# Token halves at the seams, three weight slots and roots on PSUM columns in a two-layer hybrid encoder

## The reference, cut to what matters

```python
h = rms_norm(x, ln_pre_mix[l])
m = hybrid_mixer(h, ...)       # combined projection, mixers A, B, C, D, gates, w_out
x = x + rms_norm(m, ln_post_mix[l])
h = rms_norm(x, ln_pre_ffn[l])
gu = h @ ffn_w_gu[l]
f = (silu(gu[..., :D_FF]) * gu[..., D_FF:]) @ ffn_w_down[l]
x = x + rms_norm(f, ln_post_ffn[l])
```

## Time and profile before

| | |
|---|---|
| median of 3 runs | 1854.29 us (1853.89 to 1854.39) |
| profiled execution | 1853.21 us |
| its span, first to last instruction | 1851.4 us |
| mean granted PE clock | 0.971 |
| busy: PE / DVE / ACT / POOL | 1719.6 / 921.1 / 406.1 / 1131.7 us |
| mean DMA rate | 82 GB/s |

### The profile page before, as it was taken

The page is one execution under the profiler, slowest core; times in us unless marked ns, Lnnn a source line. Parts: engine busy times, 40 slices in busy tenths (PEclk is TensorE's granted clock), DMA queues, the critical chain, the costliest instruction groups (busy, mean ns, idle before and its releaser), DMA issues.

```text
span 1851.4 us, 21177 instructions
## 1 busy us (share of the span) xinstructions
PE 1719.6 (93%) x8162; PEld 1404.2 (76%) x8162; DVE 921.1 (50%) x1621; ACT 406.1 (22%) x875; POOL 1131.7 (61%) x1172
## 2 busy tenths in 40 slices
PE   7999999899879999999879999998999699999996
PEld 6778678677667888888677787786776588888885
DVE  5755754865555333410277557558654644343102
ACT  3440313223231111100134313023332211111000
POOL 6536456343666887877584373653446668887773
PEclk9999999999989999999889999999999899999998
DMA  5112222111111222222231131121112122222221
GB/s 221 69 46 87 73 82 78 69 46 69 68 68 69 91 91 102 89 91 97 76 123 69 46 114 69 69 89 48 69 46 70 67 73 109 92 91 93 94 94 61
DMA packets 26035, 151.34 MB, mean 82 GB/s; under 512 B 3211, under 2 KB 4491, under 8 KB 12080
## 3 DMA queue, kind: packets, MB, share of 16 engines
q1 hardware_dynamic: 22176, 141.21, 21.2%
q10 hardware_dynamic: 3760, 8.78, 1.5%
HBM read 147.88 MB, written 4.70 MB: 82 GB/s over the span
## 4 chain that ended last, share of the span: by engine, by line
PE 78%; DVE 16%; issue 3%; ACT 2%; POOL 1%; DMA 0%; ACTq 0%; DVEq 0%
PE main L636 11%; PE main L533 11%; PE main L534 11%; PE main L535 11%; PE work L533 8%; PE work L534 8%; PE work L535 8%; PE turn L693 2%; PE pv L533 2%; DVE prob L1445 2%; PE pv L535 1%; PE pv L534 1%; DVE yt L1516 1%; DVE pt_lo L1229 1%; DVE tiny L1257 1%
## 5 line engine op out<-in xcount | busy, mean ns | idle before, releaser
L475 POOL TENSOR_SCALAR w_hi<-raw 128x512 fp32r<-128x512 f32 (+3 forms) x576 | 381.4, 671 | 662.5 <-issue 642.2
L479 POOL TENSOR_TENSOR w_lo<-raw,w_hi 128x512 fp32r<-128x512 f32 (+3 forms) x576 | 748.8, 1310 | 0.0
L636 PE MATMUL main<-h_hi,w_lo 128*128 128x512 f32 x512 | 208.7, 408 | 0.0
L636 PE MATMUL main<-h_hi,w_hi 128*128 128x512 f32 x512 | 208.3, 407 | 0.0
L533 PE MATMUL main<-h_hi,w_hi 128*128 128x512 f32 x480 | 192.3, 401 | 16.6 <-DVE h_lo L1231 16.0
L636 PE MATMUL main<-h_lo,w_hi 128*128 128x512 f32 x512 | 207.4, 405 | 0.0
L535 PE MATMUL main<-h_hi,w_lo 128*128 128x512 f32 x480 | 189.7, 395 | 0.0
L534 PE MATMUL main<-h_lo,w_hi 128*128 128x512 f32 x480 | 189.7, 395 | 0.0
L533 PE MATMUL work<-h_hi,w_hi 128*128 128x512 f32 x480 | 188.6, 393 | 0.0
L534 PE MATMUL work<-h_lo,w_hi 128*128 128x512 f32 x480 | 188.2, 392 | 0.0
L535 PE MATMUL work<-h_hi,w_lo 128*128 128x512 f32 x480 | 187.9, 391 | 0.0
(11 more groups left out here) (233 smaller groups left out, 3009.0 us busy)
## 6 DMA issues: line engine op xcount, KB each, us to landing
raw<-stream SPq DMA_DIRECT2D x106, 1024.0 KB, 4.8
raw<-stream SPq DMA_DIRECT2D x32, 704.0 KB, 4.1
raw<-stream SPq DMA_DIRECT2D x4, 832.0 KB, 5.0
x<-x_in ACTq DMA_DIRECT2D x4, 512.0 KB, 9.2
t_line<-t_first ACTq DMA_DIRECT2D x2, 1024.0 KB
rpb<-rpb_line ACTq DMA_DIRECT2D x32, 64.0 KB, 2.5
out<-x SPq DMA_DIRECT2D x8, 256.0 KB, 2.2
bias_b<-t_line ACTq DMA_DIRECT2D x2, 768.0 KB, 5.6
```

What stands on the lines that cost most here:

```text
L475: pool.tensor_scalar(w_hi[:, slot, parts[q]], raw[:, slot, parts[q]], 1.0, 0.0, ALU.mult, ALU.add).then_inc(piece_hi, 1)
L479: e = pool.tensor_tensor(w_lo[:, slot, part], raw[:, slot, part], w_hi[:, slot, part].bitcast(F32), ALU.subtract)
L636: mm = pe.matmul(main[m % 2][:, :], w, (h_lo if which == 1 else h_hi)[:, k, :], start=(s % STEPS == 0), stop=(s % STEPS == STEPS - 1))
```

## The change

Three things change together.

Two token parts. The eight out tiles become four whole tiles and four tiles in two halves of 256 tokens (`OUT_TILES`), all first halves before all second halves; of w_down only the last tile is halved (`DOWN_TILES`). Statistic, root, spread, residual and next input run for half 0 and then half 1. PE makes the next stage's matmuls of half 0 (of the latents, or of the FFN's first two pieces) before those of half 1. The residual goes through PSUM banks: DVE writes kept x factor and then x + that to a bank, ACT copies the bank to x and writes h_hi and the square, DVE writes h_lo from the bank. The squares of the two input norms are now added by POOL (`input_sum`, 14 additions of 128 x 256 per norm), behind the split of piece 2 and behind the split of gu1. POOL adds no x tile any more except for the output. In layer 0 the first input is made in halves too. The gate matmuls around the latents' statistic are 14 before it, 12 behind it, 22 behind the spread.

Three slots. `raw` and `w_lo` lie over each other, three slots; `w_hi` has three. SP waits for PE to be done with piece n before it loads n + 3 over it. POOL waits for the landing alone.

Roots. `token_factor` adds EPS in the PSUM bank of the statistic and works with its intermediate values in PSUM columns; only the result goes to SBUF. The latents' own root and branch C's stay in SBUF.

```diff
-    raw = sb("raw", [P, 2, 2048], F32, 48 * K)
-    w_hi = sb("w_hi", [P, 2, 2048], F32R, 64 * K)
-    w_lo = sb("w_lo", [P, 2, 2048], F32R, 80 * K)
+    raw = sb("raw", [P, SLOTS, 2048], F32, 48 * K)
+    w_lo = sb("w_lo", [P, SLOTS, 2048], F32R, 48 * K)
+    w_hi = sb("w_hi", [P, SLOTS, 2048], F32R, 72 * K)
...
+            for l in range(L):
+                for n, (name, size) in enumerate(PIECES):
+                    if n >= SLOTS:
+                        wait_freed(l, n - SLOTS)
+                    elif l:
+                        wait_freed(l - 1, NP_ + n - SLOTS)
+                    slot = n % SLOTS
+                    sp.dma_start(raw[:, slot, 0:size], stream[l * NP_ + n, :, 0:size]).then_inc(piece_in[slot], 16)
...
+            for l in range(L):
+                for n in range(3):
+                    split(l, n)
+                input_sum(l, "pre_mix")
+                for n in range(3, GU0 + 2):
+                    split(l, n)
+                input_sum(l, "pre_ffn")
+                for n in range(GU0 + 2, NP_):
+                    split(l, n)
...
+                for half in range(2):
+                    if l and half:
+                        spread(l - 1, "post_ffn", 1)
+                        pe.wait_ge(kept_done, l * N_KEPT)
+                    for k in range(KD):
...
+                        if l and half == 0 and k == 1:
+                            mean_square(l - 1, "post_ffn", 1)
+                gate_steps(l, "D", 0)
                 pe.wait_ge(loaded, 16)
-                mean_square(l, "pre_mix")
-                gate_steps(l, "D", 0)
+                input_square(l, "pre_mix")
+                gate_steps(l, "D", 1)
                 spread(l, "pre_mix")
...
+                for m in range(KD):
+                    out_tile(m)
+                out_tile(KD, range(3))
+                mean_square(l, "post_mix", 0)
+                out_tile(KD, range(3, KD))
+                out_tile(KD + 1, range(2))
+                spread(l, "post_mix", 0)
+                out_tile(KD + 1, range(2, KD))
+                out_tile(KD + 2)
+                out_tile(KD + 3)
...
                 wait_piece(l, GU0)
-                gate_up(0, 0, (0, 1), first=True)
+                for k in range(KD):
+                    first_gate_up(0, k)
+                    if k == 1:
+                        mean_square(l, "post_mix", 1)
                 wait_piece(l, GU0 + 1)
...
+                gate_up(0, 1, (0, 1), range(2), HALVES[0])
+                spread(l, "post_mix", 1)
+                gate_up(0, 1, (0, 1), range(2, KD), HALVES[0])
+                for k in range(KD):
+                    first_gate_up(1, k)
+                gate_up(0, 1, (0,), range(4), HALVES[1])
+                input_square(l, "pre_ffn")
+                gate_up(0, 1, (0,), range(4, KD), HALVES[1])
+                gate_up(0, 1, (1,), range(4), HALVES[1])
                 spread(l, "pre_ffn")
...
+                v = turn[t % 2][:, a:a + n]
+                step(l, dve.tensor_scalar(v, v, EPS, None, ALU.add))
+                root(l, n, factor_done, a, turn[t % 2])
...
+                for d in range(KD):
+                    bank = banks[d % 2][:, cols]
+                    if d >= 2:
+                        dve.wait_ge(x_kept, first + d - 1)
+                        dve.wait_ge(lo_done, at(then, N_SPLIT, SPLIT_AT[("h", to, half, d - 2)] + 1))
+                    dve.tensor_tensor(bank, kept[:, d, cols], factor(l, name, half), ALU.mult).then_inc(scaled, 1)
+                    dve.wait_ge(scaled, first + d + 1)
+                    dve.tensor_tensor(bank, x[:, d, cols], bank, ALU.add).then_inc(x_done, 1)
+                    if d:
+                        low(d - 1)
+                    if half == 0 and name == "post_mix" and d in (0, 2, 4):
+                        sum_square(l, name, KD + d // 2)
+                    if half == 0 and name == "post_ffn" and d == 4:
+                        token_factor(l, name, 1)
+                low(KD - 1)
```

More of the change, by code:

```diff
@@ L131 @@
         SPLIT += [("o", _b, _h // 2)] if _h % 2 else []
-SPLIT += [("merged", d) for d in range(KD)] + [("h", "pre_ffn", d) for d in range(KD)]
+SPLIT += [("merged", d) for d in range(KD)] + [("h", "pre_ffn", half, d) for half in range(2) for d in range(KD)]
 ACT0 = len(SPLIT)
@@ L428, in _ @@
         def _(sp):
[L429 to L447, removed]
@@ L487, in free_after @@
[L487 to L499, removed]
@@ L614, in spread @@
-            def spread(l, name):
-                t = TURN_AT[("spread", name)]
+                pe.wait_ge(summed, at(l, len(SUMMED), SUMMED_AT[(name, last - 1 if (name, last - 1) in SUMMED_AT else KD - 2)] + 1))
+                for tt in (2 * half, 2 * half + 1):
+                    pe.matmul(turn[t % 2][:, tt:tt + 1], sc["sum"][:, P * tt:P * tt + P], mean, start=tt == 2 * half, stop=False, skip_group_check=True)
+                pe.wait_ge(squared, at(l, N_KEPT, KEPT0[name] + last + 1))
+                for tt in (2 * half, 2 * half + 1):
+                    mm = pe.matmul(turn[t % 2][:, tt:tt + 1], sc["sq"][:, last % 2, P * tt:P * tt + P], mean, start=False, stop=True, skip_group_check=True)
@@ L1190, in _ @@
                     hi(l, ("merged", d), h_hi[:, d, :], merged[:, d, :], 0.5)
-                keep(l, "post_mix")
-                ffn_input(l)
+                for m in range(KD + 2):
+                    keep(l, "post_mix", m)
+                for half in range(2):
+                    for d in range(KD):
+                        next_input(l, "pre_ffn", half, d, at(l, 4 * KD, 0), x_bank)
+                        if half == 0 and d in (2, 5):
+                            keep(l, "post_mix", KD + 2 + d // 3)
                 for i in range(0, KF // 2):
@@ new lines, in factor, with first_input, residual, low @@
+            def factor(l, *name):
+                dve.wait_ge(turn_done, at(l, N_TURN, TURN_AT[("spread", *name)] + 1))
+                return turn[TURN_AT[("spread", *name)] % 2][:, HALVES[name[1]] if name[1:] else slice(0, S)]
+            def first_input():
+                for half, cols in enumerate(HALVES):
+                    for d in range(KD):
+                        lo(0, ("h", "pre_mix", half, d), h_lo[:, d, cols], x[:, d, cols], h_hi[:, d, cols], gain_in[:, 0, d:d + 1])
+            def residual(l, name, half, then, banks):
+                to, cols, kept = "pre_ffn" if then == l else "pre_mix", HALVES[half], kept_of[name]
+                first = at(l, 4 * KD, 2 * KD * (name == "post_ffn") + KD * half)
+                def low(d):
+                    gain = gain_in[:, then, d:d + 1] if to == "pre_mix" else param(to, d)
+                    lo(then, ("h", to, half, d), h_lo[:, d, cols], banks[d % 2][:, cols], h_hi[:, d, cols], gain)
+                dve.wait_ge(kept_done, l * N_KEPT + KEPT0[name] + (KD if half == 0 else len(OUT_TILES if name == "post_mix" else DOWN_TILES)))
+                for d in range(KD):
+                    bank = banks[d % 2][:, cols]
[12 more added lines that the diff above has]
+                low(KD - 1)
```

525 lines of the change are left out of this document (287 added, 238 removed).

## The result

The changed kernel takes 1840.18 us (median of 5 runs, 1839.88 to 1845.56), the kernel before in the same session 1853.89 (1852.21 to 1854.39, 5 runs). The ratio is 0.9934, 95% interval 0.992 to 0.9949: faster by 13.7 us. Forecast were 1819 and a gain of 35, in a range of 1806 to 1832. The time is outside it.

What follows compares the result with a forecast made beforehand. PE was taken as the bound, busy 1719.6 of 1851.4 us, with losses at seams, boundary, start and end. Gains 26.0 + 11.2 - 5.4 + 3.3 = 35.1 gave 1819 us, range 1806 to 1832 (8 in 10).

Steps and rivals of the forecast that it cites:

- Three slots ... steady stretches: Weight pieces away from the seams: load plus split takes 12.4 to 16 us against 21.8 available, so 0 change.
- in between PE is fed: Outside the two FFN seams, layer boundary, start and end, PE was taken not to wait.
- a term of 0.16 us: Half-width tiles on DVE: two halves cost 0.16 us more than a whole, included in the 1.27 per half tile.
- the 7.6 us from the spread to the transposes as before: Stretch from pre_mix spread to the latents' transposes, at start and boundary: taken as unchanged at 7.6 us.
- Start: Layer 0's start: POOL's half-width adds delay the statistic to 41.4 and transposes to 52.9; loss 5.4 us, bounds 0 and 8.
- Boundary: Last down tile of layer 0 to layer 1's latent transposes: 55.8 us for 68.5, gain 11.2 after 1.5 for half clock.
- FFN seam: From fourth out tile's end (A) through gate/up piece 1: gain 15.4 us, less 2.0 half clock and 0.4 weight; net 13.0 each.
- Roots: Norm roots on PSUM columns, beside a busy POOL: 11 steps in 2.3 us, bounds 2.2 and 6.4.
- End: Last down matmul to the span's end: 14.4 us for 19.7, last matmul 2.2 later; gain 3.3, bounds 1 and 5.
- Slow hand-off: Rival: half tiles crossing DVE, ACT, DVE take 1.6 us, not 1.26; seams and boundary lose about 4 each; 1831, chance 0.17.
- Slower: Rival: load and split in series after PE's release exceed 21.8 us, so weights come late; some 1920, chance 0.03.
- more standing in the attention stages: Sign that the forecast is wrong: PE waits more in the attention stages than in the kernel before; no size given.

Runs made afterwards that it cites:

- both runs on roots: Six roots per layer put back in SBUF on the changed kernel: 1870.01 us; PSUM columns for the four norm roots alone on the kernel before: 1844.1 us.

## Why the prediction was wrong, and where it was right

**The step that failed** is "Three slots ... steady stretches: **0**, cover 5 us". I put the attention at nothing because "in between PE is fed", and asked only whether PE would wait for weights. It does not: the changed kernel's waits hold no weight split, and that half of the step is right. But PE was not fed there. It already stood 19.5 us for pt_lo, so a slower DVE chain in the attention lies open on PE's path. I did not ask what POOL does to DVE when its splits move. It cost 13.4 us in the attention, 2.6 at the start and 5.0 at the boundary, of the 23.2 us by which the sum was off. The run with the slots alone (+17.9) and the one that holds the splits (0.9998) show it as the cause. I had the evidence in hand: the earlier trace rows show a short SBUF instruction that ends with POOL's, and I used that for the roots alone.

A page of the Trainium skill states this rule: "SBUF — State Buffer", section "SBUF: two separate sides", has DVE and GpSimd share a port pair as an exclusive lock, which matters to DVE instructions with two SBUF inputs (beside a GpSimd instruction that reads SBUF) or in a two-port mode. The rows agree: 294 to 442 ns with two SBUF inputs, 156 for the 128x1 RECIPROCAL in both, 0.17 us for steps with an input in PSUM. The stretched 128x8 TENSOR_SCALAR at 956.53 has one SBUF tensor as input; it would fit as the two-port case, but no row tells the mode. I had weighed the page on small tiles, a term of 0.16 us, and not this one.

**"the 7.6 us from the spread to the transposes as before"**, at the start and at the boundary, failed for the same reason: 10.2 and 12.6 us. With POOL held to out2 it is 7.3 in both.

**Start.** Statistic forecast at 41.4 for POOL's sums, measured 40.1. Transposes forecast 52.9 (the parts given, 41.4 + 13.9 - 2.8, add up to 52.5), measured 55.7. From the statistic on that is 15.6 us for 11.1 by the parts: 2.6 for the latents' root again, and nearly 2 between statistic and spread, where PE ran at half clock after its 3.96 us wait (0.43 us a matmul up to 44 us). I had no clock term here.

**Boundary.** Forecast in us behind spread 0's end S (916.4): end of w_down 3.9, half 0's latents 15.4, first h of half 1 late by 2.3, end of the latents 28.0, transposes 42.5. Measured: 4.0, 15.8, 2.6, 29.7, 48.9. The mechanism holds up to the latents' end. Half 1's 48 matmuls took 10.9 us, where 12 of half 0 had taken 2.27 (9.1 for 48): PE was at half clock for the first of them (granted 0.84 over 935.2 to 946.1), for which I had set 1.5 outside these times. The remaining 5.0 us are the latents' root.

**FFN seam.** Layer 1 took 56.3 us for the 56.4 I gave with clock and weight wait. That is luck: 2.0 of the 56.4 were for a half clock that layer 1 did not have, and slower half tiles took its place. Layer 0, which had it, took 59.1. S is at A + 16.6 (forecast 16.3), first h at S + 4.3 (4.5), the wait ahead of statistic 1 is 2.3 (2.4), spread 1 ends in layer 1 at S + 19.0 (18.6). DVE needs 1.37 us a half tile, not 1.26, since h_lo from the bank takes 0.48 and not 0.42. In layer 0 the 36 matmuls behind the gap took 6.7 us, for 4.4 in layer 1. The two stretches, with the granted clock third from the end:

```profile
548.00:562.00 14.00, 12.23 (x79) 12.18 (x80) 7.57 (x26) 4.97 (x14) 9.82 (x12) 0.76 0.15 63
1456.00:1470.00 14.00, 11.80 (x99) 11.74 (x99) 10.06 (x31) 7.16 (x20) 11.05 (x14) 1.00 0.18 71
```

The gap was 2.26 and 2.20 us. So half clock cost 2.8 us or nothing where I had set 2.0 for each, and no row says which a gap will get.

**Roots.** Forecast 2.3 us beside a busy POOL, measured 2.2 (553.02 to 555.17 in layer 0), and both runs on roots confirm it.

**End.** 4.0 us gained, forecast 3.3 (the parts given, 19.7 - 14.4 - 2.2, add up to 3.1).

**The rivals.** "Slow hand-off" gave 1831 by 1.6 us a half tile, which measured 1.37. "Slower" had the right place, the slot, with the wrong mechanism, a weight that comes late. No case priced the mechanism that decided, though I had named "more standing in the attention stages" as a sign of being wrong. So the range was too narrow on the slow side.

## What to carry to other kernels

When a change gives an engine more slots or makes it faster, write down when it will now run and what runs beside it, not only whether its consumer waits less. Where GpSimd and DVE both work in SBUF, find the DVE chains that PE waits for, and place GpSimd's bulk work between them by an explicit wait. Such a chain's values can also go to PSUM: that gave 8.5 and 30 us for the norm roots here, and nothing in the end for the latents' root while the splits stayed free. And halving a stage to overlap it halves every cover in it: count root, split and load against the shorter matmuls, piece by piece.

## What the runs showed of the hardware that was not expected

A 128x1 DVE instruction with two SBUF inputs took a mean of 282 to 480 ns over the versions, by the moment of POOL's splits; the 128x1 RECIPROCAL stayed at 155 to 157 in all of them. A 128x8 TENSOR_SCALAR from SBUF to SBUF was stretched too, to 1.16 us.

Equal gaps of PE of 2.2 to 2.3 us were followed by half clock in layer 0 and by full clock in layer 1 of the same execution, and it fell otherwise in another version with the same gaps (statistic 1 to spread 1 took 11.3 and 8.5 us in the changed kernel, 10.0 and 11.4 with the sums on DVE). This alone moves one run against another by up to 2.9 us per seam.

What becomes of 8 us saved at the latents' root while the other splits stay free is open. It was tried in two ways, with no gain and with 3.4 us.
